# Values in block products: GpSimd forms x's combinations beside K, and the samples' C and rows are loaded later

## The chip, the cores and the metric

The kernel runs on one core of a Trainium2 chip. The metric is the device time of one execution in microseconds. The kernel before takes 895.54 us, the median of 3 runs (895.25 to 895.64).

## What is computed

The kernel is one layer of a hybrid decoder, for a prompt of 512 tokens and 8 sample tokens together (520 columns). Cut to what matters here:

```
z = rmsnorm(x, g1) @ w_in                   # w_in holds q, k, v, o, the gates, u, vb, ga, gb
k = k * DK ** -0.5                          # 4 heads of 128;  v: 4 heads of 256
s = einsum('nhtk,nhsk->nhts', q, k) * Dmat  # Dmat = exp(logD - m): the decay matrix
num = einsum('nhts,nhsv->nhtv', s, v) + w_inter * einsum('nhvk,nhtk->nhtv', C, q)
C_new = decay * C + einsum('nhs,nhsv,nhsk->nhvk', w_last, v, k)
n_new = decay * n + einsum('nhs,nhsk->nhk', w_last, k)
```

All products of x with a weight are made in split precision: x and w are each the sum of a high and a low part in fp32r, and x_hi w_hi + x_lo w_hi + x_hi w_lo is summed in PSUM.

## The kernel before

**Tiles.** A projection is made in tiles ("slots") of 128 output features. One slot's weights are 128 x 1024: eight blocks of 128 x 128, one for each 128 of the 1024 input features. A tile (`tile`) takes, for each of the eight blocks, three matmuls for each half of the 520 columns: 48 matmuls of 128 x 260. The slots come in the order vb, q, u, k, v, o and then the branches, output and FFN weights. The names S_K (4 slots, one for each head), S_V (8 slots) and S_O (8 slots) stand for the first slot of K, V and O. The matmuls of all of them go through one helper line (L1961).

**Order.** Each engine has its own instruction stream, written out by hand in its own function, and they meet through semaphores. For a slot, SyncE (SP) loads the weights into one of two buffers (`raw`); ScalarE (ACT) rounds them to the high part (`split`, line "whi<-raw_pair"); VectorE (DVE) makes the low part (`low`, L1083, "wlo<-raw_pair,whi"); TensorE runs the tile into one of two PSUM banks; and ACT copies the bank to `ftmp` ("ftmp<-out"), which frees it. A slot's preparation is done one tile ahead.

**The side work of K.** In the middle of the tile after head h's, after its fourth block, TensorE makes the head's scores from `ftmp` and q ("aux<-qT,ftmp", L1961, 8 records) and four transposes ("trp<-ident,ftmp", L1995). It waits there for ACT's copy to `ftmp`. Then, in this order:

- DVE: four `d_arg` instructions (L1303: out, `nmb` and `maskmin` all in SBUF, 128 x 128 each);
- ACT: `d_exp`, four `wq`, and the copy of the transposed k (`k_tok`), then `split` of the slot after next, then `ks` and the copy of the next head's bank to `ftmp`;
- DVE: `sd` (L1306, from PSUM and SBUF), `qT<-qT,wq` (L1308, both inputs in SBUF), then `low`.

ACT's copy of the next head stands behind this head's `d_exp` in ACT's stream:

```
k_side(h - 1)
split(n.plus(2))
ready(n)
A(both(ftmp[h % 2][:, :]), out2(n), scale=DK ** -0.5)
```

**V.** Eight tiles of the same form with four transposes in the middle of the following tile. In the second tile's end come the samples' rows (`sample_rows`). From them DVE works out the samples' scalars and n, and GpSimd (POOL) writes the rows to DRAM (`scratch`), from where SP reads each back to all partitions (`row<-scratch`).

**The samples during O.** For each of the 8 samples GpSimd multiplies the state C with q (`tq`, L1893), DVE sums that and updates C, ACT makes `kv`, and SP stores the new C and loads the next one. After the last, GpSimd stages the first unit of the prompt's attention, which the first branch tile on TensorE uses (`kw`, L1904).

**Block products.** Five pairs of gate slots already use a 2 x 2 block scheme (Strassen's, in Winograd's form). `Pair` names the parts: two weight slots and two halves of the input features against the two halves of the columns, in seven products of 12 matmuls in place of eight. For this it needs four sums of weight blocks (`wsum`, by DVE) and four combinations of x's quarters (`tf`, split into `th` and `tl`). In the kernel before, DVE forms them (L1421, L1425, L1430: 128 x 1040 each) and ACT rounds them.

## Time and profile before

| what | us |
|---|---|
| median of 3 runs | 895.54 |
| the profiled execution | 896.04 |
| its span, first to last instruction | 894.2 |
| TensorE matmuls busy | 886.6 (99%) |
| VectorE busy | 609.9 (68%) |
| ScalarE busy | 390.5 (44%) |
| GpSimd busy | 133.0 (15%) |

Busy time of PE says only that matmuls were in flight, as they are pipelined: one of 128 x 260 is recorded with about 0.28 us, while the next follows after about 0.12 us. So the pitch of a run of matmuls, and the waits, tell more than the busy share. The mean granted clock of the execution is 0.996.

### The profile page before, as it was taken

To read this page: it belongs to the slowest core of one execution; us is meant where nothing else is said; L and a number is where in the kernel's file an instruction comes from. 1 tells how busy PE (TensorE), PEld (TensorE's weight loads), DVE (VectorE), ACT (ScalarE), POOL (GpSimd) and SP (SyncE) were. 2 spreads that over 40 slices of the span, in tenths; PEclk is the share of its full clock that TensorE was granted. 3 is DMA by queue.
4 is the path that set the end of the run, shared out by engine and by line. 5 is a ranking of instruction groups with operands and counts; after the bars stand their busy time and mean duration, and the time that the engine had idled before them with its cause. 6 is when DMAs were issued, how large, how long until landed. Compare 5 with 4: busy or idle time off the path is not lost.

```text
span 894.2 us, 18963 instructions
## 1 busy us (share of the span) xinstructions
PE 886.6 (99%) x7306; PEld 881.9 (99%) x7306; DVE 609.9 (68%) x980; ACT 390.5 (44%) x629; POOL 133.0 (15%) x182
## 2 busy tenths in 40 slices
PE   9999999999999999999999999999999999999997
PEld 9999999999999999999999999999999999999997
DVE  7886775443885568677755777777777778966543
ACT  7545434544873334344432344444444444432333
POOL 0673000002542110000005800000000000000001
PEclk9999999999999999999999999999999999999998
DMA  6332252234872222322255222222222222333232
GB/s 214 107 131 89 77 196 101 84 100 149 291 269 69 67 76 75 116 95 95 96 197 135 89 81 94 94 94 94 94 93 86 83 91 87 99 107 93 85 106 96
DMA packets 31499, 100.44 MB, mean 112 GB/s; under 512 B 4668, under 2 KB 7260, under 8 KB 31192
## 3 DMA queue, kind: packets, MB, share of 16 engines
q1 hardware_dynamic: 29256, 92.96, 31.1%
q0 software_dynamic: 1472, 5.72, 2.1%
q10 hardware_dynamic: 720, 1.04, 0.4%
q8 instruction: 36, 0.59, 0.3%
q14 instruction: 15, 0.12, 0.0%
HBM read 92.37 MB, written 7.35 MB: 112 GB/s over the span
## 4 chain that ended last, share of the span: by engine, by line
PE 91%; POOLq 3%; issue 3%; DMA 1%; POOL 1%; ACT 0%; SPq 0%; ACTq 0%
PE out L1961 84%; PE trp L1961 3%; PE aux L1961 2%; POOLq L1939 2%; POOLq L1937 1%; PE trp L1995 1%; DMA cwb<-in_conv_wb 1%; DMA raw_pair<-in_w_slots 1%; PE aux L2153 0%; POOL y L1952 0%; POOL out_conv_old L1923 0%; ACT xg L581 0%; POOL sct L1927 0%; POOLq L1930 0%; POOLq L88 0%
## 5 line engine op out<-in xcount | busy, mean ns | idle before, releaser
L581 ACT ACTIVATE whi<-raw_pair 128x1024 fp32r<-128x1024 f32 (+4 forms) x168 | 154.2, 924 | 207.4 <-PE out L1961 195.6
L1083 DVE TENSOR_TENSOR wlo<-raw_pair,whi 128x1024 fp32r<-128x1024 f32 (+1 forms) x121 | 155.2, 1282 | 86.8 <-ACT whi L581 86.4
L1961 PE MATMUL out<-xh,whi 128*128 128x260 f32 x668 | 143.5, 289 | 0.0
L1961 PE MATMUL out<-x2h,whi 128*128 128x260 f32 x704 | 141.8, 283 | 0.0
L1961 PE MATMUL out<-x2l,whi 128*128 128x260 f32 x704 | 141.3, 282 | 0.0
L1961 PE MATMUL out<-x2h,wlo 128*128 128x260 f32 x704 | 141.2, 282 | 0.0
L1961 PE MATMUL out<-xl,whi 128*128 128x260 f32 x668 | 139.0, 282 | 0.0
L1961 PE MATMUL out<-xh,wlo 128*128 128x260 f32 x668 | 139.0, 282 | 0.0
L1961 PEld LDWEIGHTS out<-x2h,whi 128*128 128x128 f32 x704 | 108.4, 188 | 0.1
L1961 PEld LDWEIGHTS out<-x2h,wlo 128*128 128x128 f32 x704 | 108.3, 188 | 0.0
L1961 PEld LDWEIGHTS out<-x2l,whi 128*128 128x128 f32 x704 | 108.3, 188 | 0.0
L1961 PEld LDWEIGHTS out<-xh,whi 128*128 128x128 f32 x668 | 105.2, 188 | 0.7 <-issue 0.2
L1961 PEld LDWEIGHTS out<-xl,whi 128*128 128x128 f32 x668 | 104.9, 188 | 0.0
L1961 PEld LDWEIGHTS out<-xh,wlo 128*128 128x128 f32 x668 | 104.9, 188 | 0.0
L1961 PE MATMUL out<-acth,whi 128*128 128x260 f32 (+2 forms) x266 | 58.2, 284 | 0.0
L1961 PE MATMUL out<-actl,whi 128*128 128x260 f32 (+2 forms) x266 | 57.8, 282 | 0.0
L1961 PE MATMUL out<-acth,wlo 128*128 128x260 f32 (+2 forms) x266 | 57.8, 282 | 0.0
L1645 DVE TENSOR_TENSOR up<-out,rbc 128x520 f32<-128x520 f32 x44 | 30.8, 700 | 37.5 <-PE out L1961 37.3
L1945 POOL COPY nconv<-up 128x10 f32 x44 | 10.4, 237 | 240.1 <-DVEq L1646 240.1
L581 ACT ACTIVATE acth<-silu 128x520 f32 (+1 forms) x22 | 14.1, 639 | 69.8 <-DVE silu L1660 69.8
L1961 PEld LDWEIGHTS out<-acth,whi 128*128 128x128 f32 x266 | 42.9, 188 | 0.2 <-DVE wlo L1491 0.2
L1961 PEld LDWEIGHTS out<-actl,whi 128*128 128x128 f32 x266 | 42.8, 188 | 0.0
(362 smaller groups left out, 1758.0 us busy)
## 6 DMA issues: line engine op xcount, KB each, us to landing
raw_pair<-in_w_slots SPq DMA_DIRECT2D x123, 512.0 KB, 3.3
raw_pair<-in_w_dn SPq DMA_DIRECT2D x16, 448.0 KB, 3.3
c_ring<-in_C_state SPq DMA_DIRECT2D x8, 512.0 KB, 5.1
row<-scratch SPq DMA_DIRECT2D x8, 512.0 KB, 5.9
out_C_sample<-c_ring SPq DMA_DIRECT2D x8, 512.0 KB, 4.3
raw_pair<-in_w_dn SPq DMA_DIRECT2D x8, 512.0 KB, 3.5
xres<-in_x_all POOLq DMA_DIRECT2D x1, 1560.0 KB, 6.8
x<-in_x_all SPq DMA_DIRECT2D x5, 260.0 KB, 6.7
```

The lines of the kernel that those rows point to most:

```text
L581: return act.activation(out, in_, func, **kw_)
L1083: TT(wlo[p][:, 0:width], raw[p][:, 0:width], whi[p][:, 0:width].bitcast(F32), ALU.subtract)\
L1645: TT(both(up[t][:, 2:2 + TOK]), out2(n), both(rbc2[:, :]), ALU.mult).then_inc(evac[n.c % 2], 1)
L1937: pool.drain()
L1939: pool.drain()
L1945: pool.tensor_copy(nconv[:, i * 2 + t, :], up[t][:, SEQ:2 + TOK]).then_inc(s_nc, 1)
L1961: return pe.matmul(*a, **k)
L1995: m = pe.transpose(trp[b.c % 2][:, c, :], ftmp[b.c % 2][:, c * P:(c + 1) * P], ident[:, :])
```

## The change

Four of the eight V tiles (2 with 3, and 6 with 7) are made as two pairs in seven block products each (`VPair`, `block_pair`); tiles 0, 1, 4 and 5 stay plain. The gate pairs' numbers shift by two, and so do the counts that they wait for.

The combinations of x for V are formed by GpSimd: four sums and four differences of 128 x 1040, right after GpSimd's small DMAs at the start of K. ACT rounds them during K and at V's start, and DVE makes their low parts. The products of the samples' n are given to GpSimd, while DVE keeps the small scalars. SP no longer loads the samples' C during K. C and the rows are loaded from the fourth product of the second pair on. The samples' rows are made inside V tile 1 instead of at its end. The transposes of tiles 2 and 3, and of 6 and 7, come together in the next plain tile.

```diff
@@ SP @@
+            for pr in pairs_v:
+                n0, n1, n2, n3 = pr.n
+                load(n0, wp[n0.c])
+                load(n1, wp[n1.c])
...
+            pr = pairs_v[-1]
+            sp.wait_ge(s_pd, 6 * pr.v + 4)
+            load_row(0)
+            load_state(0)
...
@@ ACT, in K @@
             for h in range(NH):
...
                 A(both(ftmp[h % 2][:, :]), out2(n), scale=DK ** -0.5).then_inc(evac[n.c % 2], 1)
+                if h == 2:
+                    v_combination_hi(0, 1)
+                if h == 3:
+                    v_combination_hi(1, 2)
+                    v_combination_hi(2, 3)
...
+            k_side(NH - 1)
+            v_combination_hi(3, 4)
+            v_plain(0)
+            first_factors_hi(pairs_v[0])
...
@@ DVE, in K @@
             for h in range(NH):
                 if h >= 1:
                     k_side(h - 1)
                 low(At(S_K + h + 2))
+            v_combination_low(0, 1)
+            v_combination_low(1, 2)
+            v_combination_low(2, 3)
             k_side(NH - 1)
...
@@ GpSimd @@
+            def x_sum(at_, k0, h):
+
+                part = (slice(None), slice(k0, k0 + KT // 2), slice(h * HALF, (h + 1) * HALF))
+                pool.tensor_tensor(vtf[:, at_, :, :], xh[part].bitcast(F32), xl[part].bitcast(F32), ALU.add)
+
+            def x_difference(to, a, b):
+
+                pool.tensor_tensor(vtf[:, to, :, :], vtf[:, a, :, :], vtf[:, b, :, :], ALU.subtract).then_inc(s_bt, 1)
+
+            pool.wait_ge(s_xn, KT)
+            x_sum(2, 0, 1)
+            x_sum(1, 0, 0)
+            pool.drain()
+            x_difference(1, 2, 1)
+            x_sum(0, KT // 2, 1)
+            pool.drain()
+            x_difference(2, 0, 2)
+            pool.drain()
+            x_difference(0, 0, 1)
+            x_sum(3, KT // 2, 0)
+            pool.drain()
+            x_difference(3, 3, 0)
...
@@ TensorE @@
+            tile(At(S_V + 1), xh, xl, mids={3: lambda: v_transposes(0), 5: sample_rows})
+            block_pair(pairs_v[0], lambda: v_transposes(1))
+            tile(At(S_V + 4), xh, xl, halves=1, mids={2: lambda: v_transposes(2), 3: lambda: v_transposes(3)})
+            tile(At(S_V + 5), xh, xl, mid=lambda: v_transposes(4))
+            block_pair(pairs_v[1], lambda: v_transposes(5))
+            tile(At(S_O), xh, xl, halves=2, mids={2: lambda: v_transposes(6), 3: lambda: v_transposes(7)})
```

GpSimd's stream at the start of K, the kernel before (`out_m_prompt` is the last small DMA, `scratch` the samples' rows, `tq` the first product of C and q):

```order
L1877 MEMSET v_tok 128x16 [waits gate_columns_done]
L1878 DMA out_m_prompt<-mrun 4x1
L1880 DMA scratch<-srows 8x1040 [waits sample_row_complete]
L1881 DMA out_n_sample<-n_s 8x512
L1882 DMA out_m_sample<-srt 8x4
```

And the changed kernel (`vtf` holds x's combinations):

```order
L2018 MEMSET v_tok 128x16 [waits gate_columns_done]
L2019 DMA out_m_prompt<-mrun 4x1
L2023 TENSOR_TENSOR vtf<-xh,xl 128x1040 [waits x_lo]
L2023 TENSOR_TENSOR vtf<-xh,xl 128x1040
L2027 TENSOR_TENSOR vtf<-vtf 128x1040
L2023 TENSOR_TENSOR vtf<-xh,xl 128x1040
L2027 TENSOR_TENSOR vtf<-vtf 128x1040 x2
L2023 TENSOR_TENSOR vtf<-xh,xl 128x1040
L2027 TENSOR_TENSOR vtf<-vtf 128x1040
L2046 TENSOR_TENSOR n_t<-n_s,srows 8x512 [waits sample_rows,sample_states_loaded]
```

Eight instructions of 128 x 1040 have come in directly behind the small DMAs. The condition on x (`x_lo`) was fulfilled long before K.

VectorE's stream at the end of K, the kernel before (from the last `low` of K's loop on; `d_arg` is the first step of the last head's side work):

```order
L1083 TENSOR_TENSOR wlo0_123<-raw_pair_120,whi0_121 128x1024 [waits w_hi]
L1303 SCALAR_TENSOR_TENSOR d_arg_68<-nmb_67,gcol,maskmin 128x128 [waits transposed]
L1303 SCALAR_TENSOR_TENSOR d_arg_68<-nmb_67,gcol,maskmin 128x128 x3
L1306 TENSOR_TENSOR sd_103<-aux,d_exp_69 128x512 [waits decay_matrix]
L1308 TENSOR_TENSOR qT_100<-qT_100,wq_137 128x512 [waits inter_weights]
```

And the changed kernel (`vtl` is the low part of the combinations):

```order
L1174 TENSOR_TENSOR wlo0_123<-raw_pair_120,whi0_121 128x1024 [waits w_hi]
L1427 TENSOR_TENSOR vtl_145<-vtf_144,vth0_146 128x1040 [waits x_combinations,x_combinations_hi]
L1427 TENSOR_TENSOR vtl_145<-vtf_144,vth1_147 128x1040 [waits x_combinations,x_combinations_hi]
L1427 TENSOR_TENSOR vtl_145<-vtf_144,vth2_148 128x1040 [waits x_combinations,x_combinations_hi]
L1393 SCALAR_TENSOR_TENSOR d_arg_68<-nmb_67,gcol,maskmin 128x128 [waits transposed]
L1393 SCALAR_TENSOR_TENSOR d_arg_68<-nmb_67,gcol,maskmin 128x128 x3
L1396 TENSOR_TENSOR sd_103<-aux,d_exp_69 128x512 [waits decay_matrix]
L1398 TENSOR_TENSOR qT_100<-qT_100,wq_137 128x512 [waits inter_weights]
```

Three instructions of 128 x 1040 now stand ahead of the last head's `d_arg`.

ScalarE's stream at the same place, the kernel before (`d_exp` of the last head to the copy of V tile 0's bank, `ftmp0`):

```order
L581 ACTIVATE d_exp_69<-d_arg_68 128x512 [waits decay_exponents]
L581 ACTIVATE wq_137<-nmb_67,mpb 128x128 x4
L581 ACTIVATE k_tok_101<-trp1 128x4x128
L581 ACTIVATE whi1_122<-raw_pair_120 128x1024 [waits slots_done,w_loaded1]
L581 ACTIVATE vs<-out1 128x8 [waits transposed,slots_done]
L581 ACTIVATE ftmp0_128<-out1 128x520
```

And the changed kernel:

```order
L638 ACTIVATE d_exp_69<-d_arg_68 128x512 [waits decay_exponents]
L638 ACTIVATE wq_137<-nmb_67,mpb 128x128 x4
L638 ACTIVATE k_tok_101<-trp1 128x4x128
L638 ACTIVATE vth3_149<-vtf_144 128x1040 [waits x_combinations]
L638 ACTIVATE vs<-out1 128x8 [waits transposed,slots_done]
L638 ACTIVATE ftmp0_128<-out1 128x520
L638 ACTIVATE whi1_122<-raw_pair_120 128x512 [waits slots_done,w_loaded1]
L638 ACTIVATE whi1_122<-raw_pair_120 128x512
```

The rounding of the last combination has taken the place of one weight slot's, and that slot's comes after the copy, as two halves.

## Rows read from the trace of the kernel before

**Rows 1.** The page's first part: busy us (share), instructions, by engine.

```profile
PE 886.6 (99%) x7306; PEld 881.9 (99%) x7306; DVE 609.9 (68%) x980; ACT 390.5 (44%) x629; POOL 133.0 (15%) x182
```

**Rows 2.** All waits of PE, first and last of four: total, times, longest.

```profile
PE aux L1961 <- DVE ones L1097: 1.2, 1, 1.2
...
PE out L1961 <- ACT whi L581: 0.5, 1, 0.5
```

**Rows 3.** Windows, K's stretch: us, busy of each engine, PEclk, DMA share, GB/s.

```profile
140.00:173.00 33.00, 33.00 (x282) 33.00 (x281) 16.80 (x36) 17.70 (x45) 2.12 (x5) 1.00 0.24 82
```

**Rows 4.** The chain that ended last, in order of time: start, us, what.

```profile
148.56 5.74 PE out L1961 x48
154.29 0.89 PE aux L1961 x8
...
161.34 0.89 PE aux L1961 x8
...
175.46 0.44 PE trp L1995 x4
```

**Rows 5.** The same chain, one stretch of a pair's and plain matmuls.

```profile
791.42 21.52 PE out L1961 x180
```

**Rows 6.** Timeline of DVE: start, us, engine, line, op, tiles, count [idle before <-releaser].

```profile
145.55 1.23 DVE L1083 TENSOR_TENSOR wlo<-raw_pair,whi 128x1024 fp32r<-128x1024 f32 x1 [1.87 <-ACT whi L581]
148.60 1.14 DVE L1303 SCALAR_TENSOR_TENSOR d_arg<-nmb,gcol,maskmin 128x128 f32<-128x128 f32 x4 [1.82 <-PE trp L1995]
...
151.61 0.69 DVE L1308 TENSOR_TENSOR qT<-qT,wq 128x512 f32<-128x512 f32 x1 [0.48 <-ACT wq L581]
...
167.15 1.23 DVE L1083 TENSOR_TENSOR wlo<-raw_pair,whi 128x1024 fp32r<-128x1024 f32 x1 [0.74 <-ACT whi L581]
169.77 1.14 DVE L1303 SCALAR_TENSOR_TENSOR d_arg<-nmb,gcol,maskmin 128x128 f32<-128x128 f32 x4 [1.40 <-PE trp L1995]
```

**Rows 7.** Timeline of ACT, from K to V tile 0.

```profile
149.77 0.63 ACT L581 ACTIVATE d_exp<-d_arg 128x512 f32<-128x512 f32 x1 [3.70 <-DVE d_arg L1303]
...
152.97 0.59 ACT L581 ACTIVATE ftmp<-out 128x520 f32<-128x520 f32 x1
...
174.14 0.59 ACT L581 ACTIVATE ftmp<-out 128x520 f32<-128x520 f32 x1
```

**Rows 8.** Timeline of POOL: its last work in K, and a large product.

```profile
145.59 0.50 POOL L1878 DMA_DIRECT2D out_m_prompt<-mrun  x1
...
201.74 2.39 POOL L1893 TENSOR_TENSOR tq<-c_ring,row 128x1024 f32<-128x1024 f32 x1 [8.19 <-DMA row<-scratch]
205.28 2.44 POOL L1893 TENSOR_TENSOR tq<-c_ring,row 128x1024 f32<-128x1024 f32 x1 [1.15 <-DMA row<-scratch]
```

**Rows 9.** Timeline of DVE, where that second product runs.

```profile
205.48 3.32 DVE L1083 TENSOR_TENSOR wlo<-raw_pair,whi 128x1024 fp32r<-128x1024 f32 x1 [4.95 <-ACT whi L581]
```

**Rows 10.** Timeline of DVE and POOL beside each other, 40.2 to 41.2 us.

```profile
40.02 1.76 POOL L1837 TENSOR_TENSOR x<-x,rbc 128x520 f32<-128x520 f32 x1
40.53 1.80 DVE L1137 SCALAR_TENSOR_TENSOR xl<-x,gains,xh 128x520 fp32r<-128x520 f32 x1
```

**Rows 11.** ACT and DVE, x's combinations for the gates (128 x 1040).

```profile
337.25 1.07 ACT L581 ACTIVATE th<-tf 128x1040 fp32r<-128x1040 f32 x1 [2.47 <-DVE tf L1425]
...
342.23 1.23 DVE L1430 TENSOR_TENSOR tl<-tf,th 128x1040 fp32r<-128x1040 f32 x1
```

**Rows 12.** PE's first instructions (timeline), and windows at the end (PE only).

```profile
1.20 4.64 PE L1961 MATMUL aux<-ones 128*128 128x128 f32 x20 [1.20 <-DVE ones L1097]
...
884.00:886.00 2.00, 1.80 (x18) 1.00 0.20 69
...
888.00:890.00 2.00, 1.61 (x8) 0.50 0.43 153
```

**Rows 13.** Timelines of POOL and PE, the end of O.

```profile
261.31 0.40 POOL L1904 TENSOR_TENSOR kw<-k_tok,wlast 128x128 f32<-128x128 f32 x1
...
263.65 0.60 PE L1961 MATMUL trp<-v_tok,sds 128*128 128x257 f32 x2
```

More of the change, by code:

```diff
@@ L63 @@
 HW = KT * P // 2
+V_PAIRS = 2
 B_VB, B_SP, B_K, B_V, B_UNIT = 0, 8, 16, 20, 28
@@ L314, in hybrid_layer @@
         pairs_w = [Pair(q) for q in range(GATE_PAIRS)]
+        pairs_v = [VPair(v) for v in range(V_PAIRS)]
         def vb_slot(j):
@@ L740, in k_side, with factor_hi, first_factors_hi, next_factors_hi @@
                 A(k_tok[:, :, h, :], trp[h % 2][:, :, :]).then_inc(tre[h % 2], 1)
+            def factor_hi(pr, f):
+                A(pr.place(whi, f), pr.factor[f]).then_inc(s_ch, 1)
+            def first_factors_hi(pr):
+                act.wait_ge(w_loaded[pr.t0], pr.n[0].half(1) * 16)
+                act.wait_ge(done, pr.n[0]())
+                factor_hi(pr, 0)
+                factor_hi(pr, 1)
+            def next_factors_hi(pr):
+                act.wait_ge(done, pr.n[1]())
+                act.wait_ge(s_sw, 4 * pr.v + 4)
+                factor_hi(pr, 2)
+                factor_hi(pr, 3)
+            def v_combination_hi(r, at):
+                act.wait_ge(s_bt, at)
+                A(vth[r][:, :, :], vtf[:, V_AT[r], :, :]).then_inc(s_th, 1)
             for h in range(NH):
@@ L775, in _ @@
-            for t in range(2):
-                v_step(0, t, True)
-            act.wait_ge(s_rowd, 1)
-            A(srows[:, 0:512], aux[0:NB, 0, :])
-            A(srows[:, 512:1024], aux[0:NB, 1, :]).then_inc(s_srow, 1)
-            act.wait_ge(s_sg, 1)
-            A(srt[:, 4:7, :], srt[:, 4:7, :], ACT.Exp).then_inc(s_sge, 1)
-            with act.Fori(1, 4) as i:
-                for t in range(2):
-                    v_step(i, t)
-            v_side(3, 1)
+                if h == 2:
+                    v_combination_hi(0, 1)
@@ L1100, in _ @@
             dve.memset(dm[:, :, :, :], 0.0).then_inc(tre[1], 1)
-            dve.memset(state[:, :, :], 0.0).then_inc(s_st, 1)
             def first_low(t, q):
@@ L1360, in _, with sample_exponents @@
-            low(At(S_V + 5))
-            with dve.Fori(2, 4) as i:
-                for t in range(2):
-                    low(At(S_V + t + 2, i, 2))
+            def sample_exponents():
+                dve.wait_ge(s_ss, 32)
+                TT(R(9), R(1), R(2), ALU.add)
+                dve.drain()
+                TT(R(3), R(9), R(0), ALU.max)
+                dve.drain()
+                TT(R(4), R(9), R(3), ALU.subtract)
+                TT(R(5), R(0), R(3), ALU.subtract)
+                TS(R(6), R(3), -1.0, None, ALU.mult).then_inc(s_sg, 1)
@@ L1365, in _ @@
+            v_next_factors(pairs_v[1])
+            v_pair(pairs_v[1])
+            dve.memset(state[:, :, :], 0.0).then_inc(s_st, 1)
             evacuated(dve, At(S_V + 7))
@@ L1961, in MM, with tile @@
                 return pe.matmul(*a, **k)
-            def tile(n, hi, lo, k0=0, nk=KT, bank=None, use=None, start=True, stop=True, mid=None, mid_at=3, each=None, end=None, mids=None):
+            def tile(n, hi, lo, k0=0, nk=KT, bank=None, use=None, start=True, stop=True, mid=None, mid_at=3, each=None, end=None, mids=None, halves=None):
                 p = n.c % 2
-                pe.wait_ge(w_lo, n(1))
+                if halves is None:
+                    pe.wait_ge(w_lo, n(1))
+                else:
+                    pe.wait_ge(s_nl, halves)
                 if start:
@@ L1972, in tile @@
                         pe.wait_ge(each, k + 1)
+                    if halves is not None and k == KT // 2:
+                        pe.wait_ge(w_lo, n(1))
                     w = slice(k * P, (k + 1) * P)
@@ L2124, in _, with product @@
             tile(At(S_V), xh, xl, mid=lambda: k_side(NH - 1))
-            tile(At(S_V + 1), xh, xl, mid=lambda: transposes(At(B_V), At(S_V)), end=sample_rows)
-            with pe.Fori(1, 4) as i:
-                for t in range(2):
-                    tile(At(S_V + t, i, 2), xh, xl,
-                         mid=lambda: transposes(At(B_V + t - 1, i, 2), At(S_V + t - 1, i, 2)))
-            tile(At(S_O), xh, xl, mid=lambda: transposes(At(B_V + 7), At(S_V + 7)))
+            def product(pr, f, o, x_hi, x_lo, first=True):
+                pe.wait_ge(s_pl, 7 * pr.v + f + 1)
+                wh, wl = pr.place(whi, f), pr.place(wlo, f)
+                for k in range(KT // 2):
+                    w = slice(k * P, (k + 1) * P)
+                    MM(o, wh[:, w], x_hi[:, k, :], start=first and k == 0, stop=False)
+                    MM(o, wh[:, w], x_lo[:, k, :], start=False, stop=False)
+                    m = MM(o, wl[:, w], x_hi[:, k, :], start=False, stop=k == KT // 2 - 1)
+                return m
@@ L2173, in _ @@
                 tile(At(S_BY + 2 * i + 1), hbh, hbl)
[L2175 to L2212 removed]
             def branch_tile(pr, hi, lo):
                 n = pr.n[2]
[L2217 removed]
+                pe.wait_ge(s_nl, pr.v + 1)
                 pe.wait_ge(evac[pr.t0], n.half(1))
```

421 lines of the change are left out of this document (257 added, 164 removed).

## The prediction

> **What bounds the kernel now.** I read the page's busy shares first. PE is at 99%, and no other engine is over 68% [rows 1]. A busy PE only says that matmuls are in flight, so I looked next at who waited: all waits of PE are four, 1.2, 0.6, 0.6 and 0.5 us, 2.9 us of 894.2 [rows 2]. The end is therefore set by the number of matmuls, until some other engine falls behind; then PE stands still and every microsecond of that is added. The windows then show the stretch that the change touches. In K (140 to 173 us) PE is full, DVE and ACT about half, and GpSimd idle but for 2.12 us [rows 3]. What has to be asked is how much room the side work has there, and that is in the chain, the timelines and the arithmetic below.
>
> **The gain.** A V tile has 48 matmuls. Two tiles have 96, a pair has 7 x 12 = 84, so two pairs take away 24. A stretch in which such a pair and plain tiles follow each other has 180 matmuls in 21.52 us, 119.6 ns each and without a wait [rows 5]. 24 x 0.1196 = 2.87 us. All transposes and sample rows stay. That is the whole of what can be won: 0.3%.
>
> **The room in K.** PE comes to the middle of a tile every 7.05 us (154.29, 161.34) and starts there with the scores, which need ACT's copy of the bank to ftmp [rows 4]. ACT starts d_exp at 149.77 and ends that copy at 152.97 + 0.59 = 153.56, 3.79 us later [rows 7]. So the chain is: transposes done, d_arg on DVE (148.60 to 149.74) [rows 6], 3.82 us of ACT with its start, PE. It is ready 0.73 us before PE wants it. Whatever delays d_arg by more than 0.73 us stops PE.
>
> **GpSimd's eight instructions.** The trace has no 128 x 1040 on GpSimd; the nearest is 128 x 1024 with two inputs, 2.39 us [rows 8], so 2.43 us each, 19.4 us for eight, with a gap of nothing (low end) to 0.15 us at a drain. GpSimd is free at 145.59 + 0.50 = 146.1 us [rows 8]. By itself this would fit into K and V. But a GpSimd instruction and a DVE instruction with both inputs in SBUF do not run at once here. DVE's low part takes 1.23 us in K [rows 6], but the one that started at 205.48, while GpSimd's product ran from 205.28 to 207.72, took 3.32 us: it ended at 208.80, 1.08 us after the product [rows 8, 9]. And they take turns. Around 40 us DVE had two xl instructions queued one behind the other. GpSimd, waiting since 40.02, got in between them (its own 1.27 us work took 1.76), and DVE's second took 1.80 in place of about 0.6 [rows 10]. Of DVE's work in K, low, each of the four d_arg and qT<-qT,wq have two SBUF inputs; sd has one.
>
> The Trainium skill says the same of the mechanism, and more ("SBUF — State Buffer", section "Who interferes with whom"): the side that issues first holds the shared port pair for its whole instruction, and a DVE instruction with one SBUF input doesn't contend. The trace agrees for one long instruction against another (3.32 us against 1.23); no row shows four short ones against a row of long ones. By that rule each of the four would wait in turn, as in the sum below; the rival "short ones slip through" is the other reading.
>
> I take strict turns, on the clock of the old trace. DVE's low of 145.55 ends at 146.78, and GpSimd's first runs to 149.21. Then one d_arg (1.14 / 4 = 0.285 us), one GpSimd instruction, and so on: the four d_arg end after three more GpSimd instructions, 149.21 + 3 x 2.43 + 4 x 0.285 = 157.64 instead of 149.74. ACT's copy ends at 157.64 + 3.82 = 161.46, and PE stands from 154.29 to there: 7.2 us.
> Next head: the fifth GpSimd instruction ends at 160.07. qT<-qT,wq (ready 1.84 us after d_exp's start, 0.69 us) [rows 6, 7] runs to 160.76, the sixth to 163.19, low to 164.42, the seventh to 166.85, one d_arg to 167.13, the eighth to 169.56, and the other three d_arg to 170.42. The copy ends at 174.24; PE had this middle at 161.34 before. So by there PE is 12.90 us late. This hardly depends on the turns inside the first head: it is the end of eight instructions and of DVE's work between them. Queued behind the blocked d_arg on DVE are sd, qT and low; on ACT behind d_exp are k_tok, the next split and the copy; PE waits for the copy. Head 2 finds GpSimd done.
>
> **The three low parts ahead of the last d_arg.** One such is 1.23 us [rows 11], about 1.16 us back to back. DVE's last low in K ends at 167.15 + 1.23 = 168.38, and three more at 171.9; the last d_arg started at 169.77 before [rows 6]: 2.1 us later. On ACT the rounding that comes in (1.07 us [rows 11]) takes the place of a split that moves behind the copy, no net cost. The copy of V tile 0's bank moves from 174.14 + 0.59 = 174.73 to 176.85 [rows 7]; PE wanted it at 175.46 [rows 4]. Cost 1.4 us, without any contention. It would be less than nothing only if PE came later, which a stall just before does not do for it, since DVE and ACT are late by the same amount. Bounds 0 and 2.1.
>
> **The clock.** PE stands still twice for over 5 us. At the kernel's end the granted clock was 1.00 in 884 to 886, while PE was full, and 0.50 (1.2 GHz) in 888 to 890, after it had had little to do [rows 12]. At the start the first 20 records took 4.64 us [rows 12]. If PE resumes at the lower level and runs so for as long, it loses half of 4.64 us, 2.3 us. After the first stall this is hidden, since PE comes early to the second one anyway; after the second it is not. Bounds 0 and 2.3; I take 1.0, the middle rounded down, as nothing shows how long the low level lasts after a stop.
> The Trainium skill ("TensorE: Matmul & The Clock Gate", section "HAM oscillation") warns of just this, a PE that idles and then restarts at half rate; by it the full 2.3 us would be due, without it 0. The end of the trace agrees that the clock falls.
>
> **The rest.** In V the pairs have the form of the gate pairs, which ran without a wait. GpSimd's five 8 x 512 products may hold DVE's small scalars up, ahead of the second pair's sums; I find the factor ready from 3 us before to 0.6 us after PE wants it. C's and the rows' loads come late, and the first two tq fall into O. The staged unit was ready at 261.31 + 0.40 = 261.71, and PE used it at 263.65 [rows 13]: 1.9 us of room, against a chain that starts some 0.4 us later (two transposes sets in the first O tile) and waits for loads that take turns. The bounds of both together are 0 and 2; I take 0.3, near 0, as room was there. SP's queue: the loads that were in K go, the ones moved stand behind the weights of tile 7 and ahead of O's third slot, which has a tile's time left. The state's memset moves on DVE to after V, where it delays only the samples' first step, within the same 1.9 us. A gain from the lighter DMA in K is excluded, as PE waited for no load there.
>
> **The sum.** -2.87 + 12.90 + 1.4 + 1.0 + 0.3 = +12.7 us. Against the profiled execution's 896.04 that is 908.8; it stood 0.5 us above the median of the runs, so 908.3 us.
>
> **Rivals.**
> 1. Short instructions slip through: the four d_arg pass together once DVE has a turn. For it: they follow each other at 0.285 us, and no row shows them being parted. Against it: rows 10. Then head 0's d_arg ends at 150.35, inside the room. Head 1's waits for the fourth GpSimd instruction: three turns with qT and low between give 159.5 to 160.65 where 156.8 was due, minus 0.73, 3.1 us; head 2's waits for the seventh likewise, 3.3 us. V tile 0's copy costs 1.8. Stops are too short for the clock. -2.87 + 3.1 + 3.3 + 1.8 + 0.3 = +5.6, so 901.1 us.
> 2. No contention, the other side: GpSimd's reads of x and of its own sums do not stop DVE (another place, other access patterns). For it: nothing in K's rows shows one. Against it: rows 9 and 10, both of plain products. Then only the 1.4 us at V tile 1 remains, -2.87 + 1.4 = -1.5, so 894.1 us. It decides at that copy: had DVE 2.1 us more room, the full gain would come, 892.7 us.
> 3. More than the sum: the clock's 2.3 us in full, and 2 us of the O chain turned into a wait of PE's first unit: 908.3 + 1.3 + 1.7 = 911.3 us.
> 4. The change doesn't do what it says: were the matmuls not fewer, all would be 2.87 us later. The order of the instructions shows 12 in each product, so I give this nothing.
>
> **How the numbers follow.** Strict turns 0.60, with its own range 905 to 911; rival 1 0.23; rival 2 0.10 (0.04 of it with the full gain); rival 3 0.07. The likeliest gives 908.3. The range goes from below rival 1 to above rival 3's sum, 899 to 912, and leaves out rival 2 and the ends, 0.15. About 0.2% (1.8 us) is what a measurement tells from no change: rival 2 lies mostly within it. Faster 0.06, same 0.06, slower 0.88.
>
> **What would show it.** In the changed kernel's waits PE should have two long ones on the scores (aux, for ACT's ftmp) in K of about 7 and 5 to 6 us, and one of about 1.4 us on the transposes in V tile 1; GpSimd's eight vtf instructions should show more than 2.43 us each where DVE came first, and DVE's first two groups of d_arg should show 8 and 4 to 6 us in place of 1.14. PEclk should fall to 0.5 in or after the stops. If d_arg keeps 1.14 us while vtf runs, contention is refuted, and with it the forecast. If the waits are three of about 3 us, rival 1 is right. If V's or O's stretch shows waits of PE of over 1 us, the rest was mis-sized.

## The result, and the profile after

The changed kernel takes **910.8 us** (median of 4 runs, 910.34 to 913.05) against 895.6 us (895.25 to 895.7, 4 runs) for the kernel before: ratio 1.0174, 95% interval 1.0162 to 1.0186. The forecast was 908.3 us, range 899 to 912, slower at 0.88. The profiled execution took 910.69 us, its span is 909.0 us (894.2 before).

The page's first part, as [rows 1]: PE has 24 instructions fewer, and is busy 1.5 us longer in a span that is 14.8 us longer.

```profile
PE 888.1 (98%) x7282; PEld 882.5 (97%) x7282; DVE 645.0 (71%) x1017; ACT 397.1 (44%) x639; POOL 159.1 (18%) x195
```

PE's waits, as [rows 2] (total, times, longest). The first three groups are new.

```profile
PE aux L2136 <- ACT ftmp L638: 7.4, 2, 6.1
PE out L2136 <- DVE wlo L1174: 4.1, 2, 3.5
PE trp L2175 <- ACT ftmp L638: 1.3, 1, 1.3
PE aux L2136 <- DVE ones L1188: 1.2, 1, 1.2
```

The first is the stop on K's scores that was forecast, the third the one in V tile 1. The second was not forecast: its 3.5 us stand in O, and the other 0.6 us stand in K, at 151.9, where PE waits for the first low part. DVE's timeline in K, as [rows 6]:

```profile
145.43 6.43 DVE L1174 TENSOR_TENSOR wlo<-raw_pair,whi 128x1024 fp32r<-128x1024 f32 x1 [1.88 <-ACT whi L638]
151.78 5.47 DVE L1393 SCALAR_TENSOR_TENSOR d_arg<-nmb,gcol,maskmin 128x128 f32<-128x128 f32 x4
...
160.54 2.83 DVE L1174 TENSOR_TENSOR wlo<-raw_pair,whi 128x1024 fp32r<-128x1024 f32 x1 [0.50 <-ACT whi L638]
164.08 4.66 DVE L1393 SCALAR_TENSOR_TENSOR d_arg<-nmb,gcol,maskmin 128x128 f32<-128x128 f32 x4 [0.71 <-PE trp L2175]
```

The same work took 1.23 and 1.14 us before. Beside it, GpSimd's row:

```profile
145.97 4.80 POOL L2023 TENSOR_TENSOR vtf<-xh,xl 128x1040 f32<-128x1040 f32 x2
151.42 2.77 POOL L2027 TENSOR_TENSOR vtf<-vtf 128x1040 f32<-128x1040 f32 x1 [0.65 <-issue]
154.14 2.44 POOL L2023 TENSOR_TENSOR vtf<-xh,xl 128x1040 f32<-128x1040 f32 x1
157.10 2.40 POOL L2027 TENSOR_TENSOR vtf<-vtf 128x1040 f32<-128x1040 f32 x1 [0.52 <-issue]
159.66 2.63 POOL L2027 TENSOR_TENSOR vtf<-vtf 128x1040 f32<-128x1040 f32 x1 [0.16 <-issue]
162.25 3.38 POOL L2023 TENSOR_TENSOR vtf<-xh,xl 128x1040 f32<-128x1040 f32 x1
```

To read it: DVE's low part ends at 151.86, 1.09 us after GpSimd's second sum (150.77), so it was held by two instructions, between which no drain stands. The first two of the four d_arg each end right behind a GpSimd instruction; the other two, about 0.3 us each, pass from 156.65 on, in and just behind the gap of 0.52 us that begins at 156.58. The second low part (160.54) came while GpSimd ran (159.66 to 162.29) and ended 1.08 us behind that one instruction, with no drain between it and the next.

Windows of PE (stretch, busy, granted clock, DMA share, GB/s), in K and in O:

```profile
155.00:160.00 5.00, 0.05 (x1) 1.00 0.01 2
160.00:165.00 5.00, 3.89 (x18) 0.53 0.12 27
165.00:170.00 5.00, 5.00 (x36) 0.78 0.20 78
170.00:175.00 5.00, 3.63 (x32) 1.00 0.14 47
...
240.00:242.00 2.00, 0.00 (x0) 1.00 0.03 12
242.00:244.00 2.00, 1.51 (x7) 0.57 0.89 324
244.00:248.00 4.00, 4.00 (x29) 0.79 1.01 352
```

After each long stop PE comes back near the lower of its two levels (1.2 GHz): 18 instructions in 3.9 us, where about 35 fit at 2.4 GHz (45 stand in the full 5 us of 175 to 180). That is why the second stop in K was only 1.4 us: PE came to it late by itself.

Where the time went is read best from starts of PE's instructions in the timelines of all kernels (us). The names of the kernels stand with the experiments.

```
kernel         scores of head 2   transposes in V 1   last V transposes (in O 0)   first unit
before         161.18             175.29              219.44                       263.65
after          172.60             188.29              229.73                       279.15
a_load_first   172.56             188.24              229.77                       278.92
a_o_fix        172.51             189.66              231.11                       275.32
c_dve          160.94             176.52              217.96                       267.83
c_order        160.96             175.07              217.50                       267.03
c_no_order     161.21             176.79              218.25                       262.47
c_all          161.33             175.44              217.82                       262.04
c_all_again    160.91             175.02              217.45                       263.40
b_sums         170.16             185.88              230.03                       274.24
b_half         163.87             179.51              223.65                       267.87
b_nodrain      179.42             193.54              237.69                       281.90
```

After less before: +11.4 us at head 2's scores (+11.5 at head 3's, 179.77 against 168.25), +13.0 in V tile 1, +10.3 at O's start, +15.5 at the first unit. So K cost 11.5, V tile 1 1.5, the pairs gave 2.7 back, and O's stretch cost 5.2: it takes 49.42 us from the last transposes to the first unit, where the kernel before has 44.21. Later 0.7 us came back; the span ends 14.8 us later.

### The profile page after: what moved, and what is told of

It reads as the page before. It is cut to its first block, busy times and chain, and to the rows that moved or that the text cites. A ratio compares the mean times of both kernels' runs of the same rounds, so it can differ in the third digit from the quotient of the medians.

```text
span 909.0 us, 18935 instructions
## 1 busy us (share of the span) xinstructions
PE 888.1 (98%) x7282; PEld 882.5 (97%) x7282; DVE 645.0 (71%) x1017; ACT 397.1 (44%) x639; POOL 159.1 (18%) x195
## 4 chain that ended last, share of the span: by engine, by line
PE 84%; issue 4%; POOLq 3%; DVE 2%; ACT 2%; DMA 2%; POOL 1%; SPq 0%; ACTq 0%; DVEq 0%
PE out L2136 78%; PE trp L2136 3%; PE aux L2136 2%; POOLq L2114 2%; DVE d_arg L1393 1%; POOLq L2112 1%; DMA raw_pair<-in_w_slots 1%; DMA cwb<-in_conv_wb 1%; PE trp L2175 1%; ACT whi L638 1%; ACT wq L638 1%; PE aux L2380 0%; DVE vtl L1427 0%; POOL y L2127 0%; DVE wv L1534 0%
## 5 line engine op out<-in xcount | busy, mean ns | idle before, releaser
L1174 DVE TENSOR_TENSOR wlo<-raw_pair,whi 128x1024 fp32r<-128x1024 f32 (+1 forms) x115 | 153.1, 1331 | 63.9 <-ACT whi L638 63.6
L2136 PE MATMUL out<-xh,whi 128*128 128x260 f32 x628 | 139.0, 292 | 4.1 <-DVE wlo L1174 4.1
L2136 PE MATMUL out<-xl,whi 128*128 128x260 f32 x628 | 134.0, 284 | 0.0
L2136 PE MATMUL out<-xh,wlo 128*128 128x260 f32 x628 | 133.9, 284 | 0.0
L2136 PEld LDWEIGHTS out<-xh,whi 128*128 128x128 f32 x628 | 101.3, 191 | 5.1 <-ACT so L638 3.7
L2136 PEld LDWEIGHTS out<-xl,whi 128*128 128x128 f32 x628 | 100.9, 191 | 0.0
L2136 PEld LDWEIGHTS out<-xh,wlo 128*128 128x128 f32 x628 | 100.5, 190 | 0.0
L2120 POOL COPY nconv<-up 128x10 f32 x44 | 10.3, 235 | 240.2 <-DVEq L1787 240.2
```

The costliest lines, as they stand in the source:

```text
L1174: TT(wlo[p][:, 0:width], raw[p][:, 0:width], whi[p][:, 0:width].bitcast(F32), ALU.subtract)\
L2120: pool.tensor_copy(nconv[:, i * 2 + t, :], up[t][:, SEQ:2 + TOK]).then_inc(s_nc, 1)
L2136: return pe.matmul(*a, **k)
```

## The experiments

All times are medians, with the kernel before run beside them (895.6 us in the first group, 895.85 in the second, 896.1 in the third).

**1. GpSimd's sums alone (b_sums).** Into the kernel before, at K's start; their result is read by nothing.

```diff
+            for _ in range(8):
+                pool.tensor_tensor(spare_sum, xh[:, 0:4, 0:256], xl[:, 0:4, 0:256], ALU.add)
+                pool.drain()
```

> The kernel before with one addition: eight GpSimd sums of 128 x 1024 (x's high and low parts, into free memory, results unused) at the start of K, where the changed kernel has its eight. Theory 1 (GpSimd's two-input instructions hold up VectorE's two-input ones; VectorE is on the path to TensorE's scores): the same loss in K without any block product, 11 us (10 to 13.5), so 905.6 to 909 us, d_arg groups of 4 to 6 us, and PE waits on ACT's ftmp of about 6 and 1 us and on wlo. Theory 2 (the loss in K comes from what else is new there, ACT's roundings, DVE's low parts or the missing C loads): within 1 us of before, 895.6 to 896.6 us.

Measured: **905.0 us** (904.51 to 905.86), ratio 1.0105 (1.0088 to 1.0121). No V tile is touched, and still PE stops on the scores:

```profile
PE aux L1965 <- ACT ftmp L582: 6.7, 2, 4.5
```

The contention costs 9.4 us by itself, below the stated 905.6 to 909 us. Read from the table as in the changed kernel, it is 10.6 us at V tile 1 (185.88 against 175.29), where the changed kernel's K has 11.5. Of the two stops, 4.5 and 2.2 us, the second was followed by half clock too. The rival without contention falls.

**2. The same time on GpSimd without reading (b_memsets).** Twenty memsets of 128 x 1024 in the same place.

```diff
+            for _ in range(20):
+                pool.memset(spare_sum[:, :, :], 0.0)
+                pool.drain()
```

> The kernel before with twenty GpSimd memsets of 128 x 1024 at the start of K, about the same busy time as the eight sums, but with nothing read. Theory 1 in its port form (the reading of SBUF by GpSimd is what blocks VectorE's second input): no loss, 895.6 us, low 1.23 us and d_arg 1.14 us as before. Rival (any work of GpSimd on SBUF holds VectorE up, or power or the semaphores do): a loss as with the sums, several us.

Measured: **895.59 us**, ratio 1.0002 (0.9992 to 1.0011), and no new wait. DVE's low part and d_arg keep their 1.23 and 1.14 us. It is not that GpSimd is busy, but that it reads. The section that I cited in the forecast (the Trainium skill, "SBUF — State Buffer", section "Who interferes with whom") says this too: a DVE instruction with two inputs in SBUF contends with a GpSimd instruction that reads SBUF, not with one that only writes it. The 0.0 us agree.

**3. The combinations earlier on GpSimd (a_early).** The eight instructions moved ahead of GpSimd's wait for the maxima, so that they run from 75 to 98 us, in Q.

```diff
             pool.tensor_tensor(acct, acct, sqt, ALU.add).then_inc(s_vss, 1)
+            pool.wait_ge(s_xn, KT)
+            x_sum(2, 0, 1)
+            ...
+            x_difference(3, 3, 0)
             pool.wait_ge(s_nmm, 1)
             ...
```

> The changed kernel with GpSimd's eight combinations moved from the start of K to behind its squares, at about 75 us, in Q, where VectorE is half idle; all else the same. Theory 1: K's two stops go (11.3 us at the middle of the third K tile), low and d_arg return to 1.23 and 1.14 us in K, and in Q less than 1.5 us is lost: 899.5 us (898.5 to 901). The stop of 1.3 us in V tile 1 and the late start of O stay. Theory 2: the time stays near 910.8 us. A gain smaller than 11 us would mean that the contention comes back in Q and U.

Measured: **914.31 us** (913.32 to 915.12), a miss by 15 us. K's stops are gone, but PE stands still for 11.8 us in Q and then runs at 0.50 of its clock (95 to 100 us). DVE's timeline there, of this kernel and then of the kernel before:

```profile
75.99 2.65 DVE L1254 TENSOR_SCALAR ig<-ig,gb 4x520 f32<-4x520 f32 x1
78.57 2.65 DVE L1256 TENSOR_SCALAR lf<-fg,gb 4x520 f32<-4x520 f32 x1
81.29 2.81 DVE L1258 TENSOR_TENSOR lf<-lf,lfe 4x520 f32<-4x520 f32 x1
84.17 9.93 DVE L1262 TENSOR_TENSOR_SCAN bcum<-ones,lf 4x128 f32<-4x128 f32 x4
...
94.69 1.20 DVE L1174 TENSOR_TENSOR wlo<-raw_pair,whi 128x1024 fp32r<-128x1024 f32 x1
```

```profile
76.28 0.47 DVE L1164 TENSOR_SCALAR ig<-ig,gb 4x520 f32<-4x520 f32 x1
...
77.99 1.36 DVE L1172 TENSOR_TENSOR_SCAN bcum<-ones,lf 4x128 f32<-4x128 f32 x4
79.93 1.20 DVE L1083 TENSOR_TENSOR wlo<-raw_pair,whi 128x1024 fp32r<-128x1024 f32 x1
```

The low part that PE needs comes 14.8 us later, because seven tiny instructions ahead of it (two TENSOR_SCALAR, one TENSOR_TENSOR, four scans) were each held by one of GpSimd's. Four scans of 0.34 us became 9.93 us. The expectation went by how much of Q DVE stood idle, and not by which instructions it had there.

**4. O's second slot loaded first (a_load_first).** SP issues it ahead of row 0 and C 0.

```diff
             sp.wait_ge(s_pd, 6 * pr.v + 4)
-            load_row(0)
-            load_state(0)
             sp.wait_ge(s_pl, 7 * pr.v + 7)
             sp.dma_start(raw[pr.t1][:, :], wp[S_O + 1]).then_inc(w_loaded[pr.t1], 16)
+            load_row(0)
+            load_state(0)
```

> The changed kernel with SP's load of O's second slot ahead of the first sample's row and C, in place of behind them; all else the same. Theory A (O's stop of 3.5 us comes from a chain that starts with this load landing late: low of that slot, state's memset, wv, kv, low of the third slot): 2 to 3 us of the stop go and with them most of the clock's loss after it, 906 to 908.5 us. Theory B (the chain waits for the samples' rows and C, which then land later still): no gain or a loss, 910.5 to 912.5 us.

Measured: **909.11 us** (907.52 to 910.93), between the two theories, 1.7 us under the changed kernel and too widely spread to count as a gain. The stop in O is still 3.4 us, and O's stretch 49.15 us (table). The trace shows why. The second slot's low part and wv do come 2.6 us earlier (227.81 and 230.11), though GpSimd still holds wv for 2.43 us. But now ACT waits until 237.87 for the third slot's weights, and their low part meets a product of GpSimd and takes 3.25 us in place of 1.22, so that it ends at 242.22, where it ended at 242.35 before. Rows of ACT, DVE and GpSimd:

```profile
237.87 1.06 ACT L638 ACTIVATE whi<-raw_pair 128x1024 fp32r<-128x1024 f32 x1 [1.47 <-DMA raw_pair<-in_w_slots]
238.97 3.25 DVE L1174 TENSOR_TENSOR wlo<-raw_pair,whi 128x1024 fp32r<-128x1024 f32 x1 [0.34 <-ACT whi L638]
238.79 2.34 POOL L2068 TENSOR_TENSOR tq<-c_ring,row 128x1024 f32<-128x1024 f32 x1 [3.81 <-DVE c_ring L1558]
```

So the second slot's load is on the way to the stop, and moving it alone does not remove the stop.

**5. DVE forms the combinations (c_dve).** The changed kernel, with the eight instructions on DVE, in its gaps, and none of them on GpSimd.

```diff
             v_stage(0, 0)
             low(At(S_Q + 5))
+            vx_sum(2, 0, 1)
+            vx_sum(1, 0, 0)
+            vx_sum(0, KT // 2, 1)
+            between = {2: lambda: vx_difference(1, 2, 1), 3: lambda: vx_difference(2, 0, 2),
+                       6: lambda: vx_difference(0, 0, 1), 7: lambda: vx_sum(3, KT // 2, 0)}
             for j in range(8):
+                if j in between:
+                    between[j]()
                 u_step(j // 2, j % 2, last=j == 7)
...
             for h in range(NH):
                 if h >= 1:
                     k_side(h - 1)
+                if h == 0:
+                    vx_difference(3, 3, 0)
                 low(At(S_K + h + 2))
```

> The changed kernel, but the eight instructions that form x's combinations (128 x 1040) are issued by DVE itself, in gaps of its row in Q, U and at K's start (three where it stood idle 4.5 us from 86.7 to 91.2 us, the others where it stood idle 1.2 to 2.4 us), and GpSimd does none of them. Theory (the K stops are GpSimd's reads of SBUF against DVE's): the two stops on the scores go, no new one comes, V tile 1 keeps its wait of 1.3 us and O its stop of about 3.5 us; 910.8 - 11.5 = 899.3 us, range 898 to 901. Rival (the work itself is too much for DVE, whoever is beside it): 8 x 1.23 = 9.8 us of more DVE work on the path, PE waits for wlo in Q or U, up to 909 us.

Measured: **900.52 us** (900.25 to 901.43), inside the stated range. The stops in K are gone and no new one came; V tile 1 keeps its 1.3 us and O a stop of 3.9 us. The first three instructions stand in a gap in which DVE had waited 4.5 us for its next low part:

```profile
86.52 3.54 DVE L1365 TENSOR_TENSOR vtf<-xh,xl 128x1040 f32<-128x1040 f32 x3
91.10 1.23 DVE L1174 TENSOR_TENSOR wlo<-raw_pair,whi 128x1024 fp32r<-128x1024 f32 x1 [1.04 <-ACT whi L638]
```

On DVE each takes 1.2 us, on GpSimd 2.4 and a hold besides. 910.8 - 900.5 = 10.3 us was the price of K's contention (11.7 us in the table, at head 2's scores).

**6. The low parts behind the last d_arg (c_order).** c_dve, and:

```diff
-            v_combination_low(0, 1)
-            v_combination_low(1, 2)
-            v_combination_low(2, 3)
             k_side(NH - 1)
...
             sample_exponents()
+            v_combination_low(0, 1)
+            v_combination_low(1, 2)
+            v_combination_low(2, 3)
+            factor_low(pairs_v[0], 2)
+            factor_low(pairs_v[0], 3)
             v_combination_low(3, 4)
-            v_next_factors(pairs_v[0])
+            first_gate_sum(pairs_v[0])
...
-                pe.wait_ge(s_tl, pr.combinations + 1)
+                pe.wait_ge(s_tl, pr.combinations + 3)
                 product(pr, 3, pr.b, *x_combination(pr, 2)).then_inc(s_pd, 1)
...
-                pe.wait_ge(s_tl, pr.combinations + 2)
+                pe.wait_ge(s_tl, pr.combinations + 3)
```

So PE's fourth and fifth products of a pair (numbers 3 and 4) now wait for three low parts of the combinations, not for one and two.

> As the kernel with DVE's combinations, and DVE's three low parts of the combinations stand behind the last head's d_arg and the pair's factors 0 and 1 instead of ahead of that d_arg. Theory (they are what makes PE wait 1.3 us in V tile 1): that wait goes and 1.3 us with it, 898.0 us, range 897 to 899.5. Rival (the low parts are then late for the pair's product 3, on DVE's queue behind the weight sums): a new wait of 1 to 3 us in the first pair, 898 to 901 us. Rival 2 (the 1.3 us are hidden by room further on): no change, 899.3 us.

Measured: **900.68 us** (898.09 to 901.21), too wide a spread to tell 1.3 us. In its trace the wait in V tile 1 is gone. What the edit gives is seen better with O in order (number 9).

**7. O's start in another order (a_o_fix).** The changed kernel, and:

```diff
+            sp.wait_ge(s_pl, 7 * pr.v + 7)
+            sp.dma_start(raw[pr.t1][:, :], wp[S_O + 1]).then_inc(w_loaded[pr.t1], 16)
             load_row(0)
             load_state(0)
-            sp.wait_ge(s_pl, 7 * pr.v + 7)
-            sp.dma_start(raw[pr.t1][:, :], wp[S_O + 1]).then_inc(w_loaded[pr.t1], 16)
             ...
             load_state(1)
+            load(At(S_O + 2), wp[S_O + 2])
             ...
             load_state(2)
-            load(At(S_O + 2), wp[S_O + 2])
...
-            dve.memset(state[:, :, :], 0.0).then_inc(s_st, 1)     # now behind the first four samples
...
-                if b >= 2:
-                    pool.wait_ge(s_cn, b)
+                pool.wait_ge(s_cn, max(b, 1))
```

> The changed kernel with O's start in another order: SP loads O's second slot before row 0 and C 0, and its third before row 2 and C 2; DVE clears the state after the first four samples; GpSimd's first product for a sample waits until DVE has written wv. Theory (O's stop comes from the third slot's weights, which stand behind six loads of rows and C, and from DVE's chain wv, kv, c_ring ahead of its low part): the stop of 3.5 us and the 2 us at half clock behind it go, 910.8 - 5.6 = 905.2 us, range 904 to 907. Rival (only the second slot's load matters, as moved alone it gave 1.7 us): 909 us. Rival 2 (what is late is the samples' chain itself, and the unit at O's end waits for it): 908 to 911 us, with the wait moved to O's end.

Measured: **908.06 us** (905.49 to 909.25), a miss by 1 us against its range. In the table O's stretch is 44.21 us again, that of the kernel before, so its 5.2 us are gone. But the profiled execution is 1.4 us later than the changed kernel's at V tile 1 (189.66 against 188.29). Its second stop in K was 1.8 us and not 1.4, and behind it the clock fell once more, to 0.60 (172.5 to 175), where the changed kernel's stayed at 1.00. Behind the first unit PE waits another 0.8 us, for ACT's hn. What the three edits give is seen better without K's stops:

**8. All three together (c_all, c_all_again).**

> All three together: DVE forms the combinations in Q, U and K's start, its low parts stand behind the last d_arg, and O's start is in the other order. If the three costs are K's contention 11.5, V tile 1's wait 1.3 and O's 5.6 us, and they add, what is left is the 24 matmuls less: 895.6 - 2.9 = 892.7 us, range 892 to 895. If O's stop is not from the order, 898 us. If DVE's work in Q and U is on the path, over 900 us.

> The same kernel as the one with all three edits, run again in five rounds for a narrower interval. Expected 894.5 us again, 893.8 to 895.5, and a ratio to the kernel before that lies under 1 with its whole interval. Rival (the 1.3 us it gained came from a low draw of runs): 895.8 us and an interval around 1.

Measured: **894.52 us** (10 runs), ratio to before 0.9987 (0.9977 to 0.9996), and again **894.79 us** (11 runs, beside 896.08), ratio 0.9989 (0.998 to 0.9998). This version beats both: 16 us under the changed kernel, 1.3 us under the one before, a small difference that came twice. It lies inside the stated 892 to 895 us, but above the 892.7 of the full gain. Against c_order it is 6.2 us, O's stop and clock (5.3 us of it in the table, 49.53 us against 44.22 for O's stretch). In the table it is 1.6 us ahead of the kernel before at the first unit, and 1.0 us of that is lost behind it. The second profile (c_all_again) stands lower at O's start, but its O stretch is 45.95 us: the fast start of O doesn't hold in every execution. Windows of PE where the changed kernel stood still:

```profile
240.00:242.00 2.00, 2.00 (x19) 1.00 0.99 389
242.00:244.00 2.00, 2.00 (x19) 1.00 0.88 361
```

And DVE's timeline there. The third slot's low part, at 241.13 in the changed kernel, comes at 225.31 in this one, and wv takes 0.22 us in place of 2.44:

```profile
217.14 0.22 DVE L1554 TENSOR_TENSOR wv<-vs,sc 128x64 f32<-128x64 f32 x1
...
225.31 1.22 DVE L1174 TENSOR_TENSOR wlo<-raw_pair,whi 128x1024 fp32r<-128x1024 f32 x1
```

**9. All but the order of the low parts (c_no_order).** c_all without the edit of number 6.

> As the one with all three edits, but DVE's three low parts of the combinations stand ahead of the last head's d_arg again, as in the changed kernel. With no stop left in K and O that could hide or blur it, theory: the wait of 1.3 us on the transposes in V tile 1 is back and costs its full length, 895.8 us, 895.3 to 896.5. Rival (in that one the pair's own waits are shorter, so it is paid back): 894.5 to 895.2 us.

Measured: **895.13 us** (11 runs) beside 894.79, ratio to before 0.999 (0.998 to 0.9999). The wait is back, and almost nothing is lost by it: 0.3 us, within the spread of either:

```profile
PE trp L2171 <- ACT ftmp L638: 1.3, 1, 1.3
```

The table shows why. In V tile 1 it is 1.35 us behind c_all (176.79 against 175.44), at O's start only 0.4 (218.25 against 217.82): with the low parts moved, c_all is 1.0 us slower in the first pair instead, in small gaps of which the profile lists one, 0.4 us on DVE's ftmp. That fits the rival: this order moves the loss and hardly lowers it. It also says where the gain went in this kernel: 2.7 us won in the pairs, less 1.5 lost in V tile 1, leaves 1.2 us.

**10. The sums without drains between them (b_nodrain).** As b_sums, written to four places in turn, and a drain only behind the fourth and the eighth.

```diff
-            for _ in range(8):
-                pool.tensor_tensor(spare_sum, ...)
-                pool.drain()
+            for _ in range(2):
+                for s in [spare_sum] + more:
+                    pool.tensor_tensor(s, ...)
+                pool.drain()
```

> The kernel before with the eight GpSimd sums (128 x 1024, read by nothing), written to four places in turn, so that no drain stands between the first four and none between the last four. Theory (a short DVE instruction slips through only where GpSimd drains; else it is held by one GpSimd instruction each): the first head's four d_arg take 10 to 11 us in place of 5.4, one stop of about 12 us on the scores, 907 to 909 us. Rival (drains don't matter, short ones slip in by chance): as with drains, 905 us, stops of 4.5 and 2.2 us. Rival 2 (DVE gets no turn until GpSimd's row of four ends): low takes over 9 us, 909 to 912 us.

Measured: **914.37 us** (913.92 to 915.11): the same eight sums cost 18.3 us in place of 9.4. DVE's timeline, and then GpSimd's:

```profile
145.48 10.97 DVE L1085 TENSOR_TENSOR wlo<-raw_pair,whi 128x1024 fp32r<-128x1024 f32 x1 [1.88 <-ACT whi L583]
156.38 9.53 DVE L1305 SCALAR_TENSOR_TENSOR d_arg<-nmb,gcol,maskmin 128x128 f32<-128x128 f32 x4
```

```profile
146.03 9.34 POOL L1883 TENSOR_TENSOR spare_sum<-xh,xl 128x1024 f32<-128x1024 f32 x4
156.02 9.74 POOL L1883 TENSOR_TENSOR spare_sum<-xh,xl 128x1024 f32<-128x1024 f32 x4 [0.65 <-issue]
```

The low part got no turn until GpSimd's four were through (155.37) and ended 1.08 us later, at 156.45. The four d_arg did take turns, one behind each of GpSimd's second four (starts 156.38, then 161.13 for the third). The time lies above all three stated ranges: the second rival had the low part right (no turn until the row of four ends) and the theory the d_arg, and the two add up. So the drains matter: the edit also writes to four places in turn, but by b_memsets writing alone holds nothing up. PE stops on the low part first, and then on the scores; behind both stops its clock is down:

```profile
PE aux L1967 <- ACT ftmp L583: 7.9, 1, 7.9
PE out L1967 <- DVE wlo L1085: 5.2, 1, 5.2
```

```profile
155.00:160.00 5.00, 3.49 (x16) 0.50 0.33 107
...
170.00:175.00 5.00, 5.00 (x24) 0.50 0.32 105
```

**11. Twice as many sums of half the size (b_half).** As b_sums, sixteen of 128 x 512, a drain behind each.

> The kernel before with sixteen GpSimd sums of half the size (128 x 512, about 1.2 us each, a drain behind each, read by nothing): the same number of elements, 19.4 us of GpSimd again. Theory A, the one of my forecast (what counts is when GpSimd's row ends, whatever the turns): DVE and PE come out as late as with eight, 905 us. Theory B (a DVE instruction is held by at most one or two of GpSimd's, so that their length sets the price): d_arg's four take about 3.5 us in place of 5.4, stops of 2.5 and 3.5 us at most, 900 to 903 us.

Measured: **900.21 us** (899.91 to 902.02): 4.1 us in place of 9.4, for the same elements. Three stops on the scores of at most 1.4 us, and no loss of clock:

```profile
PE aux L1965 <- ACT ftmp L582: 3.8, 3, 1.4
```

```profile
148.26 3.02 DVE L1304 SCALAR_TENSOR_TENSOR d_arg<-nmb,gcol,maskmin 128x128 f32<-128x128 f32 x4
...
152.82 19.92 POOL L1881 TENSOR_TENSOR spare_sum<-xh,xl 128x512 f32<-128x512 f32 x12 [0.15 <-issue]
```

Theory B holds: what counts is not when GpSimd's row ends (172.74 here, 168.55 in b_sums), but how long DVE is held each time. Halving the instructions also doubled the number of drains, and how much each of the two gives was not separated.

## Why the prediction was right, and where it was not

**The number and the sign: right.** 908.3 forecast, 910.8 measured, 2.5 us apart and inside the range, at its upper end. The mechanism that carries it, GpSimd's reads holding DVE's short instructions up and PE waiting for the scores behind them, is shown by b_sums (9.4 us with nothing else changed), by b_memsets (0.0 without the reads) and by c_dve (10.3 us back).

**The 24 matmuls, -2.87:** measured -2.7 between V tile 1 and O's start (13.0 to 10.3; c_no_order +1.5 to -1.2). Right.

**K, +12.9 and the clock +1.0:** measured 11.5 together. At head 1's scores PE was 7.0 us late (161.11 against 154.13), forecast 7.2. That is close because two errors cancel: the first low part, forecast to run ahead of GpSimd, ended 5.1 us later than forecast, and the four d_arg then took 5.5 us, and not the 8 named among the signs, as two of them passed in a drain's gap. Up to head 2's scores another 4.4 us came, forecast 5.7: 3.1 us by the lower clock (from 161.11 to where PE stood again, 171.23, are 10.1 us in place of 7.05) and a stop of 1.4. As the forecast said, the first stop's clock was hidden in front of the second stop. The second stop's clock stayed at 1.00, so the 1.0 us did not come in this execution; in a_o_fix and b_sums it did: from head 2's scores to head 3's they took 8.8 and 8.7 us, and the kernel before 7.1. The bound of 2.3 us under this term rested on the first 20 records at 4.64 us [rows 12], but the granted clock over them reads 1.00 in the trace of the kernel before, so that row shows no low level, and the 3.1 us above are what one cost.

**The reason under that size: wrong.** The forecast said that PE's lateness hardly depends on the turns, since it is the end of eight instructions and of DVE's work between. With the same elements summed, the price was 18.3 us (drains after four), 9.4 (eight drains) and 4.1 (sixteen halves). The changed kernel's first low part was held by two instructions (6.43 us), which strict turns do not allow, and that made up for the d_arg that slipped through. Without its drains the changed kernel would, by b_nodrain's 18.3, have cost several us more than strict turns give; that was not run.

**V tile 1, +1.4:** measured 1.5, a wait of 1.3 on the transposes. Right for the changed kernel. Taking the cause away gives only 0.4 us back, as c_all against c_no_order shows.

**The rest, +0.3: the mis-sized term.** It measured 5.2 us. The forecast bounded it at 2 from the unit at O's end [rows 13], and said that O's third slot had a tile's time left. It did not work out DVE's and ACT's queues ahead of that slot's low part. In the changed kernel this is read as a chain: the second slot's weights are issued at 223.16 behind row 0 and C 0, and land at 229.26; the low part and the state's memset keep wv until 232.69; there GpSimd's second product, started at 232.47, holds it, 2.44 us in place of 0.22; ACT loads a table from 235.25 and makes kv from 236.54, and the third slot's rounding stands behind that (238.90); on DVE c_ring starts at 239.03, and only then comes the third slot's low part, at 241.13. PE, due at about 239, stops for 3.5 us and then runs at 0.57 and 0.79 of its clock, which costs the other 1.7. The rows of this chain, ACT's and DVE's:

```profile
229.28 1.06 ACT L638 ACTIVATE whi<-raw_pair 128x1024 fp32r<-128x1024 f32 x1 [3.40 <-DMA raw_pair<-in_w_slots]
...
235.25 1.28 ACT L638 ACT_TABLE_LOAD   x1 [3.94 <-DVE wv L1534]
```

```profile
231.78 0.92 DVE L1527 MEMSET state<- 128x1028 f32 x1 [0.16 <-issue]
232.69 2.44 DVE L1534 TENSOR_TENSOR wv<-vs,sc 128x64 f32<-128x64 f32 x1
...
241.13 1.22 DVE L1174 TENSOR_TENSOR wlo<-raw_pair,whi 128x1024 fp32r<-128x1024 f32 x1
```

Both parts stand in the forecast, the memset "within the same 1.9 us" and a product of GpSimd that holds DVE, but it did not put them behind each other. The three edits of a_o_fix take all 5.2 away; which of them carries how much was not separated, beyond that the second slot's load alone does not (a_load_first).

So the sum came out near in part by luck: K was 2.4 us less than forecast (11.5 against 13.9), O 4.9 us more, and 0.7 us of the span was given back at its end.

**Rivals.** Slipping through (901.1 us) was half right for the d_arg and says nothing of a low part held by two. No contention falls. Of "more than the sum" one part came: O did lose, at its third slot and not at its first unit. The measured 910.8 us lies nearer to that rival's 911.3 than to 908.3.

## What to carry to other kernels

Before work is put on GpSimd because it is idle, list what DVE does in that stretch with two inputs in SBUF (and its TENSOR_SCALARs), and count each such instruction, however small, as one whole GpSimd instruction longer: seven tiny gate instructions cost 14.8 us of delay here. If it must be there, cut it into short instructions with a drain behind each (4.1 us in place of 9.4); better is DVE itself, in gaps in which the timeline shows it waiting (no new stop of PE here). And where a load or a product is moved to the start of a stage, follow each engine's queue to the second and third slot, not only to the end of the stage.

## What the runs showed that I had not expected

- A DVE instruction can be held by several GpSimd instructions that follow each other without a drain: 10.97 us, held by four, and 6.43, held by two, where 1.23 is its own time. It is not its length that decides: the low part at 160.54 got its turn behind one GpSimd instruction, though no drain stands behind that one, and so did the short d_arg in b_nodrain, 9.53 us for four. What the two held ones share is that they are recorded as starting 0.5 us ahead of GpSimd's first sum. The forecast had the side that issues first hold the ports, and two low parts of O fit that: they began at 241.13 and 246.51, 0.26 and 0.25 us ahead of a product of GpSimd, took 1.22 us, and the products took 3.21 and 3.25 us. The two held ones do not fit it. In b_sums and b_half a drain stands behind the first sum, and the like low part was held by that sum alone (4.03 and 2.95 us). Why the row holds it without a drain is open; no run was made for it.
- A DVE instruction with one tensor input can be held too: TENSOR_SCALAR on 4 x 520 took 2.65 us in place of 0.47 (its other input is a column of 4 x 1). The Trainium skill ("SBUF — State Buffer", section "Who interferes with whom") excepts the modes that use two ports, tensor_scalar's among them, from its rule on one input; these rows agree with the exception, though none names the mode.
- Granted clocks behind stops of PE in these traces: 0.57 behind 3.5 us, 0.50 behind 2.2 us (b_sums), 0.60 behind 1.8 us (a_o_fix), and 1.00 behind 1.4 us and behind all three stops on the scores in b_half (up to 1.4 us). So a stop of 2 us can cost another 1.6 us behind it.
